# Forgetting attention: values stationary in two parts, turned weights streamed, and the steps of a map regrouped

## Chip, cores and metric

One NeuronCore of a Trainium2 chip runs the whole program in one launch. The metric is device time in microseconds (us). TensorE is the matrix engine (PE in the profile; PEld its weight loads), VectorE is DVE, ScalarE ACT, GpSimd POOL, SyncE SP.

## What is computed

Two transformer blocks over 512 tokens of width 1024 in float32. The change touches one of their mixers, `odd_mixer` of the first block, with 16 heads of 64:

```python
def forgetting_attention(q, k, v, log_f):
    cum = jnp.transpose(jnp.cumsum(log_f, axis=1), (0, 2, 1))
    ...
        s = jnp.einsum('bqhd,bshd->bhqs', qb, k, preferred_element_type=jnp.float32) * scale
        s = s + (cq[..., :, None] - cum[..., None, :])
        p = masked_softmax(s, kpos[None, :] <= tpos[:, None])
        return jnp.einsum('bhqs,bshd->bqhd', p.astype(v.dtype), v)

def odd_mixer(h, w_in, b_f, w_out):
    q, k, v, f = split_cols(h @ w_in, ODD_SPLITS)
    log_f = jax.nn.log_sigmoid((f + b_f).astype(jnp.float32))
    o = forgetting_attention(...)
    return o.reshape(bsz, seq, FOX_W) @ w_out
```

Each query takes a softmax over the keys up to itself, with a bias from the summed log forget gates, and a weighted sum of the values.

## The kernel before

Activations lie transposed: the model's width on 128 partitions in 8 chunks, the 512 tokens along the free axis. Weights stream from memory in panels of 128 x 1024 through a ring. For most of them ScalarE makes a rounded high part (float32r, L567) and VectorE the low part, the rest (L571); a linear layer is then three matmuls of 512 columns for each of 8 chunks (`pe_linear_steps`, L499): high x high, high x low, low x high. `keep_up` (L550) makes the parts two panels ahead.

The stage of the forgetting attention (L1863 to L1971) works so:

- `project` (L934) makes the forget gate and, for each of 8 chunks of two heads, the projections q1, k1 and v1. VectorE drains each bank with the norm's factor (L1007). q1 and k1 are split into high and low parts that are stacked over the partitions (`act_stack_hi` L579, `dve_stack_lo` L585). v1 is turned back to tokens on partitions by four transposes (`pe_turn`, L536) and copied into `v1` by VectorE (L1037).
- The forget gate goes through three activations on ScalarE (`act_f`, L1875) and a scan and six small operations on VectorE (`dve_cum`, L1894) into `parts3`, three bfloat16 parts, whose last mark is called "lo".
- `softmax_maps` (L749) handles 64 maps (16 heads, 4 query tiles of 128). The map of query tile t has (t + 1) x 128 key columns. In step i of its programs TensorE does the scores of map i (two matmuls with stacked parts, then two bfloat16 mask matmuls), the transposes of map i - 2 (one 128 x 128 each key tile), and the value matmuls of map i - 3: turned weights are stationary (128 x 128), values of 64 columns stream, in float32. ScalarE does the turned copy (L812, every other map; VectorE L844 the others) and the exponential with its row sum (L820; the sum is read by an ACTIVATION_READ_ACCUMULATOR). VectorE does the row maximum (L832), the reciprocal of the sum (L837), and scales the output by it (L858). `pe_part` starts after `ready`, the mark "lo".
- Scores and transposes take PSUM banks 3, 4, 5 in turn (`POOLS[1]`), outputs banks 6 and 7 (`POOLS[2]`), projections 0, 1, 2. A bank is taken again once the engine that drained it is done.

`alternate` (L259) weaves the two programs on every engine by one list, `order` (L1969): the first three steps of the projections, then 6 or 9 projection steps to each 8 map steps (a projection has 3 steps, of 9, 9 and 6 matmuls), then what is left of the maps. Each engine works its list strictly in order; nothing but semaphores ties them. The projections run one pair of heads ahead of the maps and so end two heads before them. Afterwards `turned_parts` (L905) turns the output `onat1` by 32 transposes and splits it into `oT1`, and the output projection "mix1" begins (L1973).

## Time and profile before

| | |
|---|---|
| median of 3 runs | 2446.52 us (2444.91 to 2448.24) |
| profiled execution, its own time | 2448.79 us |
| its span in the trace | 2447.0 us |
| PE busy | 2374.6 us, 97% |
| PE weight loads | 1923.7 us, 79% |
| DVE busy | 1424.7 us, 58% |
| ACT busy | 1019.2 us, 42% |
| POOL busy | 273.9 us, 11% |
| mean granted clock of TensorE | 0.991 of full |

The profile is of one execution. Busy time is the union of an engine's instructions; matmuls overlap in the records, so the time that one costs in a stream is the distance from its start to the next one's start, not its recorded duration. In the rows of the trace in order of time, the bracket at the end tells how long the engine sat idle before the row and on whose account. Lines are those of the kernel before.

### The profile page before, as it was taken

To read this page: it belongs to the slowest core of one execution; us is meant where nothing else is said; L and a number is where in the kernel's file an instruction comes from. 1 tells how busy PE (TensorE), PEld (TensorE's weight loads), DVE (VectorE), ACT (ScalarE), POOL (GpSimd) and SP (SyncE) were. 2 spreads that over 40 slices of the span, in tenths; PEclk is the share of its full clock that TensorE was granted. 3 is DMA by queue.
4 is the path that set the end of the run, shared out by engine and by line. 5 is a ranking of instruction groups with operands and counts; after the bars stand their busy time and mean duration, and the time that the engine had idled before them with its cause. 6 is when DMAs were issued, how large, how long until landed. Compare 5 with 4: busy or idle time off the path is not lost.

```text
span 2447.0 us, 32007 instructions
## 1 busy us (share of the span) xinstructions
PE 2374.6 (97%) x12074; PEld 1923.7 (79%) x12086; DVE 1424.7 (58%) x2366; ACT 1019.2 (42%) x1732; POOL 273.9 (11%) x260
## 2 busy tenths in 40 slices
PE   8999899999999999999999999989999998999998
PEld 7877788888887888788888866767888776678887
DVE  3545665655655666566556469947533578666333
ACT  3666664322334444443233344444422354444323
POOL 0000111000001000100000236302100233111001
PEclk8999999999999999999999999999999999999999
DMA  4311002333432111133433312111222221102321
GB/s 180 111 54 44 1 19 104 143 133 129 143 133 87 63 59 61 53 121 129 151 125 136 117 66 70 61 35 36 95 96 97 83 70 61 44 27 75 107 95 52
DMA packets 58039, 211.77 MB, mean 87 GB/s; under 512 B 6432, under 2 KB 6560, under 8 KB 57888
## 3 DMA queue, kind: packets, MB, share of 16 engines
q1 hardware_dynamic: 57456, 208.86, 24.9%
q8 instruction: 99, 1.62, 0.3%
q10 hardware_dynamic: 432, 0.85, 0.1%
q14 instruction: 52, 0.43, 0.1%
HBM read 207.60 MB, written 2.10 MB: 86 GB/s over the span
## 4 chain that ended last, share of the span: by engine, by line
PE 83%; DVE 7%; issue 4%; ACT 4%; POOL 1%; DMA 0%; SPq 0%; ACTq 0%; DVEq 0%; POOLq 0%
PE bank L459 76%; PE last_bank L459 4%; PE bank L469 3%; DVE arena L1146 1%; DVE arena L2233 1%; DVE arena L2235 1%; DVE small L832 1%; ACT wparts L567 1%; ACT arena L820 1%; POOL rstd L626 0%; DMA cb_sb<-cb_dram 0%; DVE arena L2568 0%; DVE wparts L571 0%; ACT arena L2141 0%; DVE arena_r L585 0%
## 5 line engine op out<-in xcount | busy, mean ns | idle before, releaser
L459 PE MATMUL bank<-hT,wparts 128*128 128x512 f32 x5520 | 1334.3, 398 | 6.0 <-DMA cb_sb<-cb_dram 3.5
L459 PEld LDWEIGHTS bank<-hT,wparts 128*128 128x128 f32 x5520 | 1033.6, 190 | 237.4 <-issue 23.2
L571 DVE TENSOR_TENSOR wparts<-ring,wparts 128x1024 fp32r<-128x1024 f32 x290 | 367.3, 1267 | 422.1 <-ACT wparts L567 421.7
L459 PE MATMUL bank<-arena_r,wparts 128*128 128x512 f32 x2400 | 550.5, 390 | 0.0
L459 PEld LDWEIGHTS bank<-arena_r,wparts 128*128 128x128 f32 x2400 | 449.4, 188 | 93.8 <-DVE arena_r L601 0.8
L567 ACT ACTIVATE wparts<-ring 128x1024 fp32r<-128x1024 f32 x332 | 348.2, 1049 | 157.6 <-PE bank L459 124.1
L820 ACT ACTIVATE arena<-bank,small 128x128 f32<-128x128 f32 (+3 forms) x192 | 100.9, 526 | 143.6 <-DVE small L832 142.4
L469 PE MATMUL bank<-cf_sb,arena 128*128 128x128 f32 (+1 forms) x816 | 130.3, 276 | 15.3 <-DMA cf_sb<-cf_dram 5.4
L459 PE MATMUL last_bank<-arena 128*128 128x64 f32 x972 | 131.4, 271 | 9.6 <-DVE arena L855 4.3
L459 PEld LDWEIGHTS last_bank<-arena 128*128 128x128 f32 x972 | 122.4, 192 | 18.8 <-issue 12.6
L832 DVE TENSOR_REDUCE small<-bank 128x1 f32<-128x128 f32 (+3 forms) x192 | 93.4, 487 | 56.7 <-PE bank L459 45.1
L571 POOL TENSOR_TENSOR wparts<-ring,wparts 128x1024 fp32r<-128x1024 f32 x42 | 101.1, 2409 | 213.5 <-ACT wparts L567 213.4
L469 PEld LDWEIGHTS bank<-cf_sb,arena 128*128 128x128 f32 (+1 forms) x816 | 94.5, 145 | 30.9 <-DMA cf_sb<-cf_dram 5.4
L597 ACT ACTIVATE arena_r<-arena 128x512 fp32r<-128x512 f32 x68 | 42.9, 631 | 177.6 <-POOL arena L2792 91.4
L626 POOL TENSOR_TENSOR rstd<-hv 128x512 f32<-128x512 f32 x6 | 7.7, 1291 | 933.8 <-ACT hv L616 933.8
L459 PE MATMUL bank<-arena 128*64 128x128 f32 (+6 forms) x708 | 91.8, 330 | 14.3 <-ACT arena L820 13.9
L812 ACT ACTIVATE arena<-bank 128x384 f32<-128x384 f32 (+3 forms) x136 | 58.0, 426 | 110.3 <-PE bank L469 109.6
L1137 ACT ACTIVATE arena<-arena,vecs 128x512 f32<-128x512 f32 x44 | 35.9, 816 | 147.2 <-DVE arena L1822 147.2
L459 PEld LDWEIGHTS bank<-arena 128*128 128x128 f32 (+2 forms) x708 | 63.6, 170 | 29.9 <-ACT arena L820 16.9
L1146 DVE SCALAR_TENSOR_TENSOR arena<-arena,vecs 128x511 f32<-128x511 f32 x88 | 66.1, 751 | 16.5 <-ACT arena L1137 15.0
L459 PE MATMUL bank<-cb_sb 128*128 128x128 bf16 (+2 forms) x372 | 73.0, 251 | 0.2
L1822 DVE TENSOR_TENSOR arena<-bank,rstd 128x512 f32<-128x512 f32 x44 | 30.4, 691 | 66.4 <-PE bank L459 62.1
(277 smaller groups left out, 2123.3 us busy)
## 6 DMA issues: line engine op xcount, KB each, us to landing
ring<-weights_dram SPq DMA_DIRECT2D x388, 512.0 KB, 3.4
arena<-x_dram SPq DMA_DIRECT2D x4, 512.0 KB, 6.3
out_dram<-arena SPq DMA_DIRECT2D x4, 512.0 KB, 4.0
rot<-rot_dram SPq DMA_DIRECT2D x1, 512.0 KB, 10.9
rot<-rot_dram ACTq DMA_DIRECT2D x1, 512.0 KB, 3.2
cf_sb<-cf_dram SPq DMA_DIRECT2D x1, 416.0 KB, 9.3
cb_sb<-cb_dram SPq DMA_DIRECT2D x1, 264.0 KB, 10.1
vecs<-vec_dram ACTq DMA_DIRECT2D x1, 258.5 KB, 6.3
```

Source lines behind the costliest of these rows:

```text
L459: i = pe.matmul(*args, **kw)
L469: i = pe.transpose(*args)
L567: eng.activation(wparts[:, slot, 0, :, :], ring[:, p % RAW, :, :], ACT.Copy)\
L571: eng.tensor_tensor(wparts[:, slot, 1, :, :], ring[:, p % RAW, :, :], wparts[:, slot, 0, :, :].bitcast(F32), ALU.subtract)\
L597: act.activation(dst, src, ACT.Copy).then_inc(*act_made.mark((key, "hi")))
L812: act.activation(PT[:, j % 3, 0:W], banks[key, "t", j][:, 0:W], ACT.Copy)\
L820: act.activation(Pb[:, i % 3, 0:W], banks[key, "s", i][:, 0:W], ACT.Exp, bias=mx(i), accum_out=sm(i)).then_inc(*act_made.mark((key, "p", i)))
L832: dve.tensor_reduce(mx(i), banks[key, "s", i][:, 0:W], AX.X, ALU.max, negate=True)\
L1137: act.activation(cv, src, ACT.Identity, bias=b, scale=w).then_inc(*act_made.mark((key, "tap", n)))
L1146: dve.scalar_tensor_tensor(out=cv[:, s:SEQ], in0=src[:, 0:SEQ - s], scalar=w, in1=cv[:, s:SEQ], op0=ALU.mult, op1=ALU.add)\
L1822: dve.tensor_tensor(an[:, n % 3, :], banks[(key, "a"), n][:, :], scale, ALU.mult)\
L2233: dve.max(tops[:, r, :], sc).then_inc(*dve_made.mark((K + "top", qt, r)))
```

## The change

Values are now stationary and split. The transposed v1 is copied twice: ScalarE makes its high part (L991 of the new file), VectorE the low part; they lie beside each other (high, low for one head; low, high for the other, `v1[..., 2 * side:2 * side + 2, :]`), in a ring of three chunks. The exponentials are scaled by the reciprocal on GpSimd before they are transposed (`pool_fox`). The turned weights of a head's four maps are split into a high part (ScalarE) and a low part (VectorE) and kept for the whole head. For each head there are then eight matmuls in one bank, two for each key tile kt, with the 128 columns of split values stationary and 512 - 128 kt query columns streamed. The two halves of the bank's partitions hold the parts of the output; ScalarE moves one half across (`swap1`), VectorE adds the other and writes the transposed output `o1`. The turning of the output at the end goes; `oT1` is split from `o1`. Step i is now: transposes of map i - 3, values of a head (where i mod 4 is 3), masks, scores of map i; the other engines treat what TensorE made one step earlier. The exponentials lie in `hv`, the gate's parts in `rstd`.

```diff
@@ project: the values' turning, ScalarE and VectorE @@
+                elif it["kind"] == "turn" and "low" in it:
+                    act.wait_ge(*filled[it["key"], "nat", it["n"]])
+                    if it["free"] is not None:
+                        act.wait_ge(*it["free"])
+                    act.activation(it["dst"], by_head(it["key"], it["n"]), ACT.Copy)\
+                       .then_inc(*act_made.mark((it["key"], "turned hi", it["n"])))
...
+                elif it["kind"] == "turn" and "low" in it:
+                    dve.wait_ge(*act_made[key, "turned hi", n])
+                    dve.tensor_tensor(it["low"], by_head(key, n), it["dst"].bitcast(F32), ALU.subtract)\
+                       .then_inc(*dve_made.mark((key, "turned", n)))
+                    banks.drain((key, "nat", n), "dve_made")
...
-        fox = softmax_maps("fox", maps, Pb1, PT1, lambda i: small_cols(32, i), lambda i: small_cols(36, i, 6),
-                           [dve_made["lo"]], *POOLS[1:])
-        order = [0, 0, 0] + spread(6, 8) + spread(9, 8) * (KD - 2) + [0] + [1] * (len(maps) + 3)
-        then(turned_parts("ot1", onat1, oT1, [dve_made["fox", "out", 63]]))
...
+        def pe_fox(pe):
+            pe.wait_ge(*dve_made["lo"])
+            for i in range(M1 + 5):
+                if 3 <= i < M1 + 3:
+                    j = i - 3
+                    n = j % NT + 1
+                    pe.wait_ge(*pool_made["fox", "scaled", j])
+                    bank = banks.take(pe, ("fox", "t", j), S1)
+                    for t in range(n):
+                        tp(pe, bank[:, t * P:(t + 1) * P], Pb1[:, j % 3, t * P:(t + 1) * P], ident,
+                           done=("fox", "t", j) if t == n - 1 else None)
+                if i >= 7 and i % NT == 3:
+                    h = (i - 7) // NT
+                    c, side = divmod(h, 2)
+                    pe.wait_ge(*dve_made["fox", "lo", NT * h + NT - 1])
+                    pe.wait_ge(*dve_made["v1", "turned", c])
+                    bank = banks.take(pe, ("fox", "o", h), O1)
+                    for kt in range(NT):
+                        values = v1[:, c % VRING, kt, 2 * side:2 * side + 2, :].rearrange("p b d -> p (b d)")
+                        for part in range(2):
+                            last = (kt, part) == (NT - 1, 1)
+                            mm(pe, bank[:, kt * P:SEQ], lhsT=values, rhs=fox_moving(h, part, kt), start=(kt, part) == (0, 0),
+                               stop=last, done=("fox", "o", h) if last else None)
+                if i < M1:
...
+        def act_fox(act):
+            for i in range(M1 + 5):
+                if 3 <= i < M1 + 3:
+                    j = i - 3
...
+                    act.activation(fox_turned(j, 0), turned_map(j), ACT.Copy).then_inc(*act_made.mark(("fox", "hi", j)))
+                if 1 <= i < M1 + 1:
+                    j = i - 1
...
+                    act.activation(Pb1[:, j % 3, 0:W], banks["fox", "s", j][:, 0:W], ACT.Exp, bias=mx1(j),
+                                   accum_out=sm1(j)).then_inc(*act_made.mark(("fox", "p", j)))
+                    banks.drain(("fox", "s", j), "act_made")
+                if i >= 8 and i % NT == 0:
...
+                    act.activation(swap1[HALF[side], :], banks["fox", "o", h][HALF[1 - side], :], ACT.Copy)\
+                       .then_inc(*act_made.mark(("fox", "swap", h)))
+                yield
...
+        def pool_fox(pool):
+            for i in range(M1 + 5):
+                if 2 <= i < M1 + 2:
+                    j = i - 2
+                    p = Pb1[:, j % 3, 0:maps[j]["width"]]
+                    pool.wait_ge(*dve_made["fox", "inv", j])
+                    pool.tensor_scalar(p, p, sm1(j), None, ALU.mult).then_inc(*pool_made.mark(("fox", "scaled", j)))
+                yield
```

`dve_fox` does in step i the maximum of map i - 1, the reciprocal of map i - 2, the low part of the turned map i - 3, and, every fourth step, the sum of a head's halves.

TensorE, in the third pair of heads while projections run; `bank<-arena_r` of 128 to 512 columns are scores, `arena 128x64` values, `L469` transposes, `hT,wparts` projections. Before, two steps:

```order
L459 MATMUL bank<-arena_r 128x384 x2
L459 MATMUL bank<-arena,cb_sb 128x384
L459 MATMUL bank<-cb_sb 128x128
L469 MATMUL bank<-cf_sb,arena 128x128
L459 MATMUL last_bank<-arena 128x64 x4
L459 MATMUL bank<-hT,wparts 128x512 x9
L459 MATMUL bank<-arena_r 128x512 x2
L459 MATMUL bank<-arena,cb_sb 128x512
L459 MATMUL bank<-cb_sb 128x128
L469 MATMUL bank<-cf_sb,arena 128x128 x2
L459 MATMUL bank<-arena 128x64
L459 MATMUL bank<-hT,wparts 128x512 x9
```

Now one step with a head's values between transposes and scores:

```order
L472 MATMUL bank<-cf_sb,hv 128x128
L462 MATMUL last_bank<-arena_r 128x512 x2
L462 MATMUL last_bank<-arena_r 128x384 x2
L462 MATMUL last_bank<-arena_r 128x256 x2
L462 MATMUL last_bank<-arena_r 128x128 x2
L462 MATMUL bank<-rstd,cb_sb 128x512
L462 MATMUL bank<-cb_sb 128x128
L462 MATMUL bank<-arena_r 128x512 x2
L462 MATMUL bank<-hT,wparts 128x512 x9
```

The 64-column matmuls of every step have become one burst in every fourth, ahead of that step's scores.

ScalarE at the start of the stage, before (L579 the stacks of k1, L1877 to L1881 the forget gate):

```order
L579 ACTIVATE arena_r<-arena 64x512 [waits dve_made]
L579 ACTIVATE arena_r<-arena 64x512 x3
L1877 ACTIVATE arena<-arena 16x512 [waits dve_made]
L1879 ACT_TABLE_LOAD
L1879 ACTIVATE arena<-arena 16x512 [waits act_made]
```

and now:

```order
L585 ACTIVATE arena_r<-arena 64x512 [waits dve_made]
L585 ACTIVATE arena_r<-arena 64x512 x3
L991 ACTIVATE arena_r<-bank 128x4x2x64 [waits bank_filled]
L1913 ACTIVATE arena<-arena 16x512 [waits dve_made]
L1915 ACT_TABLE_LOAD
L1915 ACTIVATE arena<-arena 16x512 [waits act_made]
```

The values' high part, which waits for TensorE's transposes, has come ahead of the gate's activations.

VectorE in the same third pair, now (L2086 maximum, L2091 reciprocal, L2095 low part of a turned map, L2102 sum of the halves, L1049 low part of the values):

```order
L2086 TENSOR_REDUCE small<-bank 128x1 [waits act_made,bank_filled]
L2091 RECIPROCAL small<-small 128x1 [waits act_made]
L2095 TENSOR_TENSOR arena_r<-bank,arena_r 128x2x128 [waits act_made]
L2102 TENSOR_TENSOR arena<-bank,hv 64x512 [waits act_made]
L1049 TENSOR_TENSOR arena_r<-bank,arena_r 128x4x128 [waits act_made]
L2086 TENSOR_REDUCE small<-bank 128x1 [waits act_made,bank_filled]
L2091 RECIPROCAL small<-small 128x1 [waits act_made]
```

Between one map's maximum and its reciprocal now lie the low part of an earlier map, the head's sum and the next map's maximum.

## Rows read from the trace of the kernel before

**Rows 1.** The page, busy time, share of the span and instructions of each engine.
```profile
PE 2374.6 (97%) x12074; PEld 1923.7 (79%) x12086; DVE 1424.7 (58%) x2366; ACT 1019.2 (42%) x1732; POOL 273.9 (11%) x260
```

**Rows 2.** Busy time by window: stretch, length, engines, clock, DMA share, GB/s.
```profile
850.00:900.00 50.00, 50.00 (x300) 41.76 (x298) 33.86 (x74) 24.14 (x53) 0.00 (x0) 1.00 0.16 54
```

**Rows 3.** TensorE in order of time, middle: start, length, line, operation, tiles, count.
```profile
851.15 1.00 PE L459 MATMUL last_bank<-arena 128*128 128x64 f32 x8
851.96 2.33 PE L459 MATMUL bank<-hT,wparts 128*128 128x512 f32 x9
854.13 0.62 PE L459 MATMUL bank<-arena_r 128*128 128x512 f32 x2
854.59 0.39 PE L459 MATMUL bank<-arena,cb_sb 96*128 96x512 bf16 x1
```

**Rows 4.** TensorE in order of time, the stage's end.
```profile
982.30 0.65 PE L469 MATMUL bank<-cf_sb,arena 128*128 128x128 f32 x4 [1.12 <-DVE arena L1007]
...
987.83 0.39 PE L459 MATMUL bank<-arena,cb_sb 96*128 96x512 bf16 x1
...
994.71 0.39 PE L459 MATMUL bank<-arena,cb_sb 96*128 96x512 bf16 x1
...
999.74 3.71 PE L469 MATMUL bank<-cf_sb,arena 128*128 128x128 f32 x32 [0.38 <-DVE arena L858]
...
1003.21 12.97 PE L459 MATMUL bank<-arena_r,wparts 128*128 128x512 f32 x56
```

**Rows 5.** VectorE's groups by form, 820 to 980: busy us, mean ns, idle before.
```profile
L585 DVE TENSOR_TENSOR arena_r<-arena,arena_r 64x512 fp32r<-64x512 f32 x36 | 24.7, 686 | 9.3 <-ACT arena_r L579 8.6
L571 DVE TENSOR_TENSOR wparts<-ring,wparts 128x1024 fp32r<-128x1024 f32 x17 | 20.8, 1225 | 12.9 <-ACT wparts L567 12.9
...
L832 DVE TENSOR_REDUCE small<-bank 128x1 f32<-128x512 f32 x11 | 7.6, 692 | 2.3 <-PE bank L459 2.1
L837 DVE RECIPROCAL small<-small 128x1 f32<-128x1 f32 x46 | 7.2, 156 | 0.3
...
L858 DVE TENSOR_SCALAR arena<-bank,small 128x64 f32<-128x64 f32 x23 | 6.4, 277 | 0.0
```

**Rows 6.** ScalarE's groups by form, 820 to 980.
```profile
L579 ACT ACTIVATE arena_r<-arena 64x512 fp32r<-64x512 f32 x36 | 22.5, 626 | 0.6
L567 ACT ACTIVATE wparts<-ring 128x1024 fp32r<-128x1024 f32 x17 | 17.8, 1049 | 0.0
L820 ACT ACTIVATION_READ_ACCUMULATOR arena<-bank,small 128x1 f32 x46 | 8.9, 194 | 0.0
L820 ACT ACTIVATE arena<-bank,small 128x512 f32<-128x512 f32 x11 | 7.6, 689 | 22.3 <-DVE small L832 22.3
...
L812 ACT ACTIVATE arena<-bank 128x384 f32<-128x384 f32 x11 | 5.4, 491 | 11.2 <-PE bank L469 11.2
```

**Rows 7.** Instructions of line 2017: ns min/median/max, first and last start us.
```profile
L2017 POOL TENSOR_SCALAR xT<-xT,vecs x8: 1564/1748/1886, 1458.3 to 1488.6; 128x512 f32<-128x512 f32 x8
```

**Rows 8.** All engines in order of time, the stage's start.
```profile
783.29 0.63 ACT L1877 ACTIVATE arena<-arena 16x512 f32<-16x512 f32 x1
...
785.86 0.66 PE L469 MATMUL bank<-cf_sb,arena 128*128 128x128 f32 x4 [0.79 <-DVE arena L1007]
...
787.18 0.63 ACT L1881 ACTIVATE arena<-arena 16x512 f32<-16x512 f32 x1
...
787.84 0.68 DVE L1896 SCALAR_TENSOR_TENSOR arena<-arena 16x512 f32<-16x512 f32 x1 [0.60 <-ACT arena L1881]
...
792.92 0.44 PE L459 MATMUL bank<-arena_r 128*128 128x128 f32 x2 [0.92 <-DVE arena L1913]
```

**Rows 9.** TensorE in order of time, a wait in the second block.
```profile
1529.38 0.40 PE L459 MATMUL bank<-rstd,cf_sb 16*128 16x64 f32 x2 [3.19 <-DVE arena L1146]
```

**Rows 10.** Busy time by window, the stretch behind that wait.
```profile
1529.40:1533.00 3.60, 3.60 (x12) 2.90 (x13) 3.46 (x14) 2.47 (x7) 2.05 (x1) 0.59 0.00 0
```

**Rows 11.** VectorE in order of time, beside GpSimd's work in the second block.
```profile
1464.56 1.41 DVE L1167 TENSOR_TENSOR arena<-arena,rot 128x512 f32<-128x512 f32 x1
```

More of the change, by code:

```diff
@@ L41 @@
 DSA_EVERY = 4
+VRING = 3
+FOX_STEP = SEQ - P
+FOX_PART = FOX_STEP * (NT - 1) + SEQ
 ALL_BANKS = tuple(range(NBANK))
@@ L1959, in build @@
                     qk=[(qs1[:, at, qt * P:W], kh1[:, at, 0:W]), (qs1[:, at, qt * P:W], kl1[:, at, 0:W])], width=W,
[L1960 to L1963 removed]
+                    masks=[(cstb("selneg")[0:96, h:h + 1].to_broadcast([96, P]), parts3[0:96, 0:W], 0),
+                           (identb, cstb("causal"), qt * P)],
@@ L1971, in build, with mx1, sm1, turned_map @@
-        then(turned_parts("ot1", onat1, oT1, [dve_made["fox", "out", 63]]))
+                            act_made["k1", c, side, "hi", 1 - side])))
+        M1 = len(maps)
+        S1, O1 = POOLS[1:]
+        def mx1(i):
+            return small_cols(32, i)
+        def sm1(i):
+            return small_cols(36, i, 6)
+        def turned_map(i):
+            W = maps[i]["width"]
+            return banks["fox", "t", i][:, 0:W].rearrange("p (t w) -> p t w", w=P)
+        def pe_fox(pe):
[22 more added lines that the diff above has]
+                if i < M1:
+                    m = maps[i]
+                    for w in m["before"]:
+                        pe.wait_ge(*w)
+                    bank = banks.take(pe, ("fox", "s", i), S1)
+                    for n, (a, b, c) in enumerate(m["masks"]):
+                        mm(pe, bank[:, c:c + b.shape[-1]], lhsT=a, rhs=b, start=n == 0, stop=False)
+                    for n, (q, k) in enumerate(m["qk"]):
+                        mm(pe, bank[:, 0:m["width"]], lhsT=q, rhs=k, start=False, stop=n == 1,
+                           done=("fox", "s", i) if n else None)
+                yield
@@ L1972, in build, with act_o1, dve_o1 @@
+        def act_o1(act):
+            act.wait_ge(*filled["fox", "s", M1 - 1])
+            for k in range(KD):
+                act.wait_ge(*dve_made["fox", "out", 2 * k + 1])
+                act_hi(act, oT1[:, 0, k, :], o1[:, k, :], ("ot1", k))
+        def dve_o1(dve):
+            for k in range(KD):
+                dve_lo(dve, oT1[:, 0, k, :], oT1[:, 1, k, :], o1[:, k, :], ("ot1", k))
+        then(act=act_o1, dve=dve_o1)
         f1 = Norm("f1", 1, ("ffn_norm", 1), filled["v1", KD - 1])
```

81 lines of the change are left out of this document (68 added, 13 removed).

## The prediction

> **What bounds the kernel now.** I read the page first: TensorE is busy 97% of the span [rows 1]. Then the stages in the table of windows: in the forgetting-attention stage, while projections run between the heads, it is busy 50.00 of 50.00 us, VectorE 33.86 and ScalarE 24.14, at full clock [rows 2]. So there the sum of TensorE's work sets the time. Then TensorE in order of time through the stage's end: the last block of projection work ends at 982.30, the last two heads follow alone, and the output projection starts at 1003.21 [rows 4]. In that stretch 20.9 us pass and TensorE waits in places: no other work covers the softmax's chain. Last, the stage's beginning: TensorE waits 0.92 us for the forget-gate sums [rows 8]. What the change is worth thus hangs on three places: start, interleaved middle, uncovered end.
>
> **Values: fewer, longer matmuls.** Before, each head has 10 pairs of tiles (query tile by key tile), every one recorded as 2 instructions of 64 columns, 20 in all. Eight of them take from 851.15 to 851.96, 0.10 us each [rows 3]; a head 1.9 to 2.0 us. Now a head has 8 matmuls, two each of 512, 384, 256 and 128 columns, in the same rounded format as the scores. The score pair of 512 takes 0.46 us (854.13 to 854.59) [rows 3]; by columns the four pairs make 0.46 x 1280/512 = 1.15, with a little for the small ones 1.2. Saved: 0.7 us a head, 11 us for 16 heads, all on the engine that bounds the middle. Gone too are the 32 transposes of the output, 3.5 us from 999.74 to 1003.21 [rows 4], but they stand in the uncovered end, where the chain decides. Moving the masks ahead of the scores costs nothing: same matmuls, same bank.
>
> **Other engines.** For each pair of heads VectorE loses a value copy, four turned copies and eight 0.28 us output scalings; it gets the low part of the values, eight low parts of the weights and two sums. Copies, low parts and sums are priced by the nearest row, a 512-wide operation from PSUM at 0.69 [rows 5], about 0.55, 0.4 and 0.28 when narrower. That is 0.69 + 2 x (0.4 + 0.69) + 8 x 0.28 = 5.1 us gone, 0.69 + 2 x 1.92 + 2 x 0.69 = 5.9 added in a period of two heads, 27 us (seven of them from 792.92 to 982.30 [rows 4, 8]): VectorE goes from 68% to some 73%. ScalarE gets four more copies, the values' high part and two moves of 0.63 [rows 6], 3.5 us. GpSimd, idle here, gets eight scalings. Its one row of that form has 1.56 us at least, 1.75 median and 1.89 at most for 512 columns [rows 7]; I take 1.57, and for the narrower maps, between that and a share by columns, 1.2, 0.85, 0.5. None is full. By throughput alone the change gains 11 us.
>
> **The chain is longer.** Before, a map's transposes wait for maximum and exponential only. Now they wait for maximum, exponential, reciprocal and GpSimd's scaling, and each engine's program is in order. In the widest map of a head (512) the path from its scores to its transposes is: 0.2 (TensorE's matmuls are recorded to end 0.16 after the next can start, 0.62 against 0.46 [rows 3]), maximum 0.69 [rows 5], exponential 0.69 + 0.19 [rows 6], then on ScalarE the move of the previous head's half output 0.63, on VectorE the sum that waits for it 0.69, only then the next map's maximum 0.28 and this map's reciprocal 0.16, GpSimd 1.57: 5.1 us, 5.3 with hand-overs of 0.04 (787.18 + 0.63 to 787.84 [rows 8]). The sum stands ahead of the reciprocal in VectorE's program; that is the costly place.
>
> **Middle.** Between those scores and those transposes TensorE has three blocks of projection (two of 9 and one of 6 matmuls: 851.96 to 854.13 is 2.17 for nine [rows 3], so 5.8) and 1.3 of small maps: 7.1 us of cover. But VectorE and ScalarE do the projection's own work in the same queues: the high and low parts of a weight panel (1.05 and 1.23), a drained bank 0.69, and for a key projection four splits of 0.69 [rows 5, 6]. 5.3 + 1.05 + 1.23 + 0.69 = 8.3 against 7.1: a wait of 1.2, more beside the key splits, none where no panel falls between. Laying the steps of one period of two heads out by these durations I get waits of 2 to 3 us in all, most before the transposes of the widest maps, against 1.4 saved. Over seven periods: from -10 (all covered) to +10 (2.9 us of wait each). Where consecutive VectorE instructions overlap a little the waits shrink; I take +0.6 a period, **+4**.
>
> **Start.** The values' high part is now ScalarE's, and its program has it ahead of the three activations of the forget gate. Before, these began at 783.29 and ended at 787.81; the transposes that the high part waits for start at 785.86, so it can begin at 786.5 and end at 787.15, and only then comes the gate's chain. It moves by 3.9 us, and with it VectorE's sums and the first map, for which TensorE waited already [rows 8]: **+3.9**, a wait of 4.8 us. None of it is hidden. After a wait of 3.19 us elsewhere [rows 9] the granted clock of the stretch behind is 0.59 of full over 3.6 us, near the lower level of 1.2 GHz [rows 10]: half speed for about 3.4 us costs 1.7. **+1.7**; ends 0 and 2.
>
> **End.** A cycle of one head without cover, before: 987.83 to 994.71, 6.88 us [rows 4]. After: 5.3 to the end of the scaling, transposes 0.44, +0.2, high part of the turned weights 0.6 (the 384 copy is 0.49 [rows 6]), then ScalarE's next exponential, some 0.47 + 0.19 for 256 columns, which frees the bank for the next transposes, 0.15, the head's value matmuls 1.2, scores of the next widest map 0.75 (0.46 and masks of 512 and 128 columns, a matmul each, 0.29): 9.3 us. Two cycles: +4.8. Drain: before, from the last scores at 995.0 to the output projection 8.2 us; after, 5 to the scaling's end, 0.44, high 0.6, low 0.69, values 1.2, move 0.63, sum 0.69, low part of the first chunk 0.6, hand-overs 0.6: 10.4, so +2.2, although the turning is gone. Entry: TensorE leaves its last projection with the chain about 3 us behind. Together **+10**; ends +6 (scaling at 60% of my price, no swap in the way) and +13 (the clock falls here too).
>
> **Sum:** +4 + 3.9 + 1.7 + 10 = +19.6. The profiled execution took 2448.79 us outside a span of 2447.0; the median shown is 2446.52, 2.3 less. From the median 2466. A measurement can tell 0.2%, about 5 us.
>
> **Rivals.**
> 1. *The middle is covered.* VectorE's 73% leaves room, and a late reciprocal is caught up under three projection blocks. Then -10 + 5.6 + 10 = +6: 2452. It speaks for it that TensorE had no waits in the middle before; against it, that ScalarE and VectorE wait for each other twice per head now.
> 2. *Faster: TensorE binds everywhere.* If the in-order chain keeps pace (it decides at about 4.5 us from scores to transposes, against my 5.3), a head in the end costs TensorE's own 1.2 + 1.1 + 2.2 = 4.5 (values, ten transposes of 0.11, scores with masks) instead of 6.9, -5, and the middle -10, with the start at +3.9: -11, 2436. Against it: GpSimd's row, which no wait shortens.
> 3. *The engines' memory port.* A VectorE instruction with two SBUF inputs of 512 columns took 1.41 us while GpSimd worked [rows 11], and 0.69 in this stage with GpSimd idle [rows 5]. The panel and key splits are of that form and now run beside GpSimd's scalings. Two meetings a period at half a microsecond each add up to 7: 2473. The Trainium skill (SBUF — State Buffer, on the shared port pair) calls it an exclusive lock, held for a whole instruction, against a GpSimd instruction that reads SBUF; by that rule the trace agrees, and it speaks against this change.
> 4. *The change doesn't do what it says:* the values' matmuls cost no less, since each needs its weights loaded anew for a 128 part; 0.7 x 14 more in the middle at worst: 2476.
>
> **Chances.** Forecast 0.49, rival 1 0.17, rival 2 0.14, rival 3 0.13, rival 4 0.07. Faster by over 0.2%: rival 2, 0.14. Within 0.2%: the lower half of rival 1 and a little of rival 2's border, 0.11. Slower 0.75. The forecast's own range is 2458 to 2474; to leave out no more than 2 in 10 it must reach below rival 1, to 2446, and to 2477 above.
>
> **What would show it.** The first map's scores about 4 us later, with TensorE waiting on VectorE for some 4.8 us; behind it a low granted clock. Value matmuls near 1.2 us a head, in one burst. In the middle, waits of TensorE's transposes on GpSimd. At the end about 31 us from the last value transposes to the output projection instead of 20.9, cycles of about 9 us, ScalarE's move and VectorE's sum between the maximum and the reciprocal. The prediction is wrong if the middle shows TensorE without waits and a period near 26, or an end near 21.

## The result, and the profile after

The changed kernel takes **2466.73 us** (median of 4 runs, 2465.69 to 2467.43), the kernel before 2447.38 on the same chip (4 runs, 2444.91 to 2449.39): a ratio of 1.0079, 95% interval 1.0062 to 1.0097, 19.35 us slower. The profiled executions have spans of 2464.5 and 2447.0 us and mean clocks of 0.985 and 0.991. The page of the changed kernel, against [rows 1]:

```profile
PE 2373.0 (96%) x11862; PEld 1915.7 (78%) x11862; DVE 1430.6 (58%) x2350; ACT 1048.0 (43%) x1788; POOL 343.0 (14%) x324
```

The page alone explains nothing: TensorE has 212 instructions fewer and is busy 1.6 us less, although part of its work now runs at the lower clock. So I cut the stage at four places that both traces have: the first value transposes of the stage, the first map's first matmul, the last value transposes, and the first matmul of the output projection.

| stretch | before | after | difference | predicted |
|---|---|---|---|---|
| start: first value transposes to first map | 7.06 (785.86 to 792.92) | 10.94 (783.21 to 794.15) | +3.9 | +3.9 |
| middle: to the last value transposes | 189.38 (to 982.30) | 190.01 (to 984.16) | +0.6, of it 1.5 to 1.7 the low clock | +4, and 1.7 for the clock |
| end: to the output projection | 20.91 (to 1003.21) | 34.62 (to 1018.78) | +13.7 | +10 |
| behind: first stretch of the output projection | 5.76 | 7.67 | +1.9 | 0 |

The low clock's share of the middle is 1.7 by the window below (0.42 of its 4.00 us) and 1.5 by the run e1. The row behind runs from the output projection's first matmul to its first drained bank. The four sum to 20.1. That is more than the 17.5 between the spans because the stage begins 2.65 us earlier in this execution. The program ahead of it is the same; what differs there is the granted clock of the first 100 us, 0.91 before and 0.97 now (in the run e10 it was 0.91 too, and the stage began at 785.25).

**Start.** All engines in order of time; columns: start, length, engine, line, operation, tiles, count, in brackets idle time before and what ended it. Against [rows 8]:

```profile
783.21 0.66 PE L472 MATMUL bank<-cf_sb,arena 128*128 128x128 f32 x4 [0.78 <-DVE arena L1019]
...
783.91 0.60 ACT L991 ACTIVATE arena_r<-bank 128x512 fp32r<-128x512 f32 x1 [3.27 <-PE bank L472]
784.53 0.63 ACT L1913 ACTIVATE arena<-arena 16x512 f32<-16x512 f32 x1
...
788.42 0.63 ACT L1917 ACTIVATE arena<-arena 16x512 f32<-16x512 f32 x1
...
794.15 0.29 PE L462 MATMUL bank<-rstd,cb_sb 96*128 96x128 bf16 x1 [4.82 <-DVE rstd L1949]
...
794.77 3.56 PE L462 MATMUL bank<-hT,wparts 128*128 128x512 f32 x9
```

ScalarE idles 3.27 us for the transposes, then makes the values' high part, then begins the gate at 784.53. TensorE's wait is 4.82 us instead of 0.92. Behind it nine projection matmuls take 3.56 us, where nine took 2.33 [rows 3], and the window says why:

```profile
794.20:798.20 4.00, 4.00 (x14) 3.11 (x15) 3.09 (x4) 0.88 (x3) 0.00 (x0) 0.58 0.39 131
```

(length, busy time of PE, PEld, DVE, ACT, POOL with counts, granted clock, DMA share, GB/s.) The clock is 0.58 of full in this window, where it was 1.00 in the same window before: mostly the lower level, 1.2 GHz.

**Middle.** TensorE in order of time, the end of a head's values, its next widest scores, and the transposes of that map; this answers to [rows 3]:

```profile
966.63 1.47 PE L462 MATMUL last_bank<-arena_r 128*128 128x512 f32 x8
967.94 0.39 PE L462 MATMUL bank<-rstd,cb_sb 96*128 96x512 bf16 x1
...
968.74 2.25 PE L462 MATMUL bank<-hT,wparts 128*128 128x512 f32 x9
...
971.39 1.61 PE L462 MATMUL bank<-hT,wparts 128*128 128x512 f32 x6
...
973.63 2.21 PE L462 MATMUL bank<-hT,wparts 128*128 128x512 f32 x9
976.48 0.66 PE L472 MATMUL bank<-cf_sb,hv 128*128 128x128 f32 x4 [0.64 <-POOL hv L2113]
```

The eight value matmuls hold TensorE for 1.31 us (966.63 to 967.94) instead of 1.9. The transposes of the widest map wait 0.64. TensorE's waits from 796 to 984 (us, times, longest); before, there were two waits of 1.4 us together, both in the first heads (801.82 and 803.31), and none from there to 982:

```profile
PE bank L472 <- POOL hv L2113: 8.7, 14, 1.4
```

A period of two heads is 27.83 before and 27.76 now. In a steady period TensorE idles twice, 0.45 and 0.64 us. The run e3 below, without any of these waits, has a period of 26.26: TensorE's own work fell by 1.57 us a period, and the waits put 1.50 back, 0.4 more than the records show as idle time. Of the work saved, the bursts are 0.6 us a head. The rest is about what the projections gain: nine of their matmuls hold TensorE for 2.09 us behind scores (968.74 to 970.83), where behind 64-column matmuls it was 2.17 [rows 3], six times a period.

**End.** TensorE from the last value transposes on, against [rows 4]:

```profile
984.16 0.66 PE L472 MATMUL bank<-cf_sb,arena 128*128 128x128 f32 x4 [0.79 <-DVE arena L1019]
...
995.68 0.39 PE L462 MATMUL bank<-rstd,cb_sb 96*128 96x512 bf16 x1
...
998.83 0.88 PE L472 MATMUL bank<-cf_sb,hv 128*128 128x128 f32 x3 [1.63 <-ACT hv L2074]
...
1001.75 1.12 PE L472 MATMUL bank<-cf_sb,hv 128*128 128x128 f32 x4 [1.19 <-POOL hv L2113]
...
1004.28 2.14 PE L462 MATMUL bank<-arena_r 128*128 128x512 f32 x8
1006.26 0.39 PE L462 MATMUL bank<-rstd,cb_sb 96*128 96x512 bf16 x1
...
1013.95 2.61 PE L462 MATMUL last_bank<-arena_r 128*128 128x512 f32 x8 [1.41 <-DVE arena_r L2095]
1018.78 1.62 PE L462 MATMUL bank<-arena_r,wparts 128*128 128x512 f32 x3 [2.22 <-DVE arena_r L607]
```

A head's cycle without cover is 10.58 us (995.68 to 1006.26) instead of 6.88. Inside it, VectorE, ScalarE and GpSimd on the widest map and the head's sum:

```profile
996.68 0.69 DVE L2086 TENSOR_REDUCE small<-bank 128x1 f32<-128x512 f32 x1 [2.36 <-PE bank L462]
...
997.41 0.69 ACT L2065 ACTIVATE hv<-bank,small 128x512 f32<-128x512 f32 x1
...
998.21 0.59 ACT L2074 ACTIVATE hv<-last_bank 64x512 f32<-64x512 f32 x1
...
998.83 0.69 DVE L2102 TENSOR_TENSOR arena<-last_bank,hv 64x512 f32<-64x512 f32 x1 [1.06 <-ACT hv L2074]
...
999.56 0.29 DVE L2086 TENSOR_REDUCE small<-bank 128x1 f32<-128x128 f32 x1
...
999.88 0.16 DVE L2091 RECIPROCAL small<-small 128x1 f32<-128x1 f32 x1
...
1000.14 2.14 POOL L2113 TENSOR_SCALAR hv<-hv,small 128x512 f32<-128x512 f32 x2 [1.36 <-DVE small L2091]
```

The order is as predicted: maximum, exponential, ScalarE's move, VectorE's sum, the next map's maximum, and only then the reciprocal that GpSimd waits for. From the widest maximum's start to the transposes 5.07 us pass (996.68 to 1001.75), and from the end of its scores (996.48) 5.27, against 5.3 in the prediction. The last row joins two scalings, 512 columns and the 128 of the next map. And the clock, in the end and behind it:

```profile
984.16:1018.78 34.62, 20.04 (x89) 15.54 (x90) 14.43 (x37) 14.45 (x37) 11.42 (x10) 0.71 0.00 0
1018.78:1061.00 42.22, 42.22 (x178) 34.76 (x179) 22.62 (x27) 18.02 (x28) 6.50 (x5) 0.95 0.27 88
```

Before, both clocks were 1.00. In shorter windows the clock falls behind the wait of 2.86 us before 988.23 (0.54 from 988.23 to 995.68), is back at 1.00 from 995.68, falls again behind the wait of 1.63 (0.51 from 998.83 to 1001.75), is back at 1.00 from 1006.26, and is 0.50 from 1013.95 to 1022.50, behind waits of 1.97, 1.92 and 1.41. Before the change, waits of up to 1.12 us stood in this stretch. Now 89 matmuls take 20.04 us of the end; four transposes 1.12 us instead of 0.66, eight value matmuls 2.14 instead of 1.47.

### The profile page after: what moved, and what is told of

Its sections match the earlier page's. It is cut to its first block, busy times and chain, and to the rows that moved or that the text cites. A ratio compares the mean times of both kernels' runs of the same rounds, so it can differ in the third digit from the quotient of the medians.

```text
span 2464.5 us, 31535 instructions
## 1 busy us (share of the span) xinstructions
PE 2373.0 (96%) x11862; PEld 1915.7 (78%) x11862; DVE 1430.6 (58%) x2350; ACT 1048.0 (43%) x1788; POOL 343.0 (14%) x324
## 4 chain that ended last, share of the span: by engine, by line
PE 82%; DVE 7%; issue 5%; ACT 4%; POOL 2%; DMA 0%; SPq 0%; ACTq 0%; DVEq 0%; POOLq 0%
PE bank L462 75%; PE last_bank L462 4%; PE bank L472 3%; DVE arena L1163 1%; POOL hv L2113 1%; DVE arena L2392 1%; DVE arena L2394 1%; ACT wparts L573 1%; POOL rstd L632 0%; ACT arena L826 0%; DVE small L838 0%; DVE arena L1019 0%; DMA ring<-weights_dram 0%; DVE small L2086 0%; DVE arena L2727 0%
## 5 line engine op out<-in xcount | busy, mean ns | idle before, releaser
L462 PE MATMUL last_bank<-arena 128*128 128x64 f32 x780 | 107.0, 273 | 8.0 <-DVE arena L861 4.4
L462 PEld LDWEIGHTS last_bank<-arena 128*128 128x128 f32 x780 | 99.3, 194 | 16.7 <-issue 11.5
L472 PE MATMUL bank<-cf_sb,arena 128*128 128x128 f32 (+4 forms) x624 | 99.7, 280 | 11.6 <-DMA cf_sb<-cf_dram 5.0
L826 ACT ACTIVATE arena<-bank,small 128x256 f32<-128x256 f32 (+3 forms) x128 | 67.2, 525 | 73.4 <-DVE small L838 72.8
L2113 POOL TENSOR_SCALAR hv<-hv,small 128x128 f32<-128x128 f32 (+1 forms) x64 | 69.3, 1083 | 180.0 <-DVE small L2091 180.0
L472 PEld LDWEIGHTS bank<-cf_sb,arena 128*128 128x128 f32 (+4 forms) x624 | 74.9, 148 | 23.0 <-DMA cf_sb<-cf_dram 5.0
L462 PE MATMUL bank<-arena 128*64 128x128 f32 (+6 forms) x580 | 74.0, 346 | 14.3 <-ACT arena L826 13.6
L838 DVE TENSOR_REDUCE small<-bank 128x1 f32<-128x256 f32 (+3 forms) x128 | 62.3, 487 | 40.3 <-PE bank L462 39.3
L818 ACT ACTIVATE arena<-bank 128x256 f32<-128x256 f32 (+3 forms) x104 | 45.7, 439 | 70.1 <-PE bank L472 69.4
L607 DVE TENSOR_TENSOR arena_r<-arena,arena_r 128x512 fp32r<-128x512 f32 x76 | 53.1, 707 | 35.6 <-ACT arena_r L603 35.4
```

Of the source, the lines that this page charges most:

```text
L462: i = pe.matmul(*args, **kw)
L472: i = pe.transpose(*args)
L607: dve.tensor_tensor(lo, src, hi.bitcast(F32), ALU.subtract).then_inc(*dve_made.mark((key, "lo")))
L818: act.activation(PT[:, j % 3, 0:W], banks[key, "t", j][:, 0:W], ACT.Copy)\
L826: act.activation(Pb[:, i % 3, 0:W], banks[key, "s", i][:, 0:W], ACT.Exp, bias=mx(i), accum_out=sm(i)).then_inc(*act_made.mark((key, "p", i)))
L838: dve.tensor_reduce(mx(i), banks[key, "s", i][:, 0:W], AX.X, ALU.max, negate=True)\
```

## The experiments

Each is an edit of the changed kernel. "Ratio" is to the kernel before on the same chip, with its 95% interval; the changed kernel's own is 1.0079. The runs e1 to e4 stood beside a kernel before of 2445.59 us, e5 to e8 of 2449.60, e9 and e10 of 2449.24, so of two medians the ratios tell more than the difference. The intervals of e1, e2, e4, e5 and e7 overlap that of the changed kernel: what such an edit gives back is read from the stretches of its trace, one execution each, and the medians only agree with it. The last columns are read from each run's trace as in the table above: the first to the last value transposes (start and middle together), a period of two heads, and the end.

| run | median us | ratio | start and middle | period | end |
|---|---|---|---|---|---|
| kernel before | 2447.38 | 1 | 196.44 | 27.83 | 20.91 |
| changed kernel | 2466.73 | 1.0079 | 200.95 | 27.76 | 34.62 |
| e1 gate first | 2461.35 | 1.0059 (1.0040 to 1.0079) | 195.53 | 27.75 | 35.81 |
| e2 sum late | 2460.41 | 1.0061 (1.0040 to 1.0082) | 196.35 | 26.98 | 30.77 |
| e3 no scaling | 2453.64 | 1.0032 (1.0022 to 1.0041) | 191.54 | 26.26 | 30.26 |
| e4 warm end | 2460.45 | 1.0059 (1.0039 to 1.0080) | 200.97 | 27.74 | 31.05 |
| e5 VectorE scales in the end | 2463.29 | 1.0073 (1.0048 to 1.0098) | 202.05 | 27.75 | 30.12 |
| e6 VectorE scales | 2458.14 | 1.0045 (1.0029 to 1.0062) | 193.31 | 26.26 | 32.54 |
| e7 scores first | 2467.01 | 1.0083 (1.0067 to 1.0098) | 202.57 | 27.83 | 35.80 |
| e8 together | 2446.80 | 0.9994 (0.9984 to 1.0003) | 186.79 | 26.30 | 27.49 |
| e9 together, warm end | 2442.36 | 0.9969 (0.9956 to 0.9982) | 186.76 | 26.30 | 25.20 |
| e10 distances of before | 2454.98 | 1.0026 (1.0016 to 1.0035) | 197.57 | 27.85 | 24.63 |

### e1: the gate ahead of the values' high part

The gate's activations and sums are run before the first value item's copies instead of after them.

```diff
                            free=filled["fox", "o", 2 * (c - VRING) + 1] if c >= VRING else None,
+                           **(dict(act2=act_f, dve2=dve_cum) if c == 0 else {}))]
...
-        then(act=act_f, dve=dve_cum)
```

> Only the start changes: ScalarE does the forget gate's activations, and VectorE its sums, before the two parts of the first turned values. Theory (the start's order costs 3.9 us of wait and 1.7 us of low clock): the wait before the first map's masks falls from 4.82 us to about 1, the granted clock stays full behind it, and the whole runs 5 to 6 us faster than the changed kernel, some 2461. Rival (the wait is taken back later, because the middle is bound by the other engines' chain and TensorE would wait there anyway): the start gets 4 us shorter and the middle 4 us longer, 2466.

```profile
783.41 0.63 ACT L1917 ACTIVATE arena<-arena 16x512 f32<-16x512 f32 x1
783.94 0.57 ACT L991 ACTIVATE arena_r<-bank 128x512 fp32r<-128x512 f32 x1
...
789.14 0.23 PE L462 MATMUL bank<-rstd,cb_sb 96*128 96x128 bf16 x1 [0.94 <-DVE rstd L1949]
```

The wait before the first map is back at 0.94 and start and middle together are 5.4 us shorter: 3.9 of chain and 1.5 of clock, 5.6 predicted. The period doesn't move. In this execution the end is 1.2 longer, at a clock of 0.62; the median is 5.4 lower (4.9 by the ratios) all the same. The start's term stands, in the traces.

### e2: the sum of the halves one map later

```diff
-            for i in range(M1 + 5):
+            for i in range(M1 + 6):
...
-                if i >= 8 and i % NT == 0:
-                    h = (i - 8) // NT
+                if i >= 9 and i % NT == 1:
+                    h = (i - 9) // NT
```

(In VectorE's program alone; ScalarE's move stays.)

> VectorE's sum of a head's two halves moves one step later, behind the next reciprocal. Theory (the sum, waiting for ScalarE's move, holds up the reciprocal and with it GpSimd's scaling of the widest map): that map's scaling starts about 1.3 us earlier, the waits of TensorE on GpSimd in the middle (8.7 us, 14 times) nearly go, the end gets 2 to 3 us shorter; together 8 to 11 us, some 2457. Rival (GpSimd's own 1.56 us and the longer path as such are what costs; the queue order only shifts the wait): less than 2 us.

No work is taken away, only its place in one queue: 4.6 us less in the middle (the waits on GpSimd go from 8.7 to 4.9), 3.9 less in the end, the median 6.3 lower (4.4 by the ratios; the profiled execution was the fastest of the five). The forecast of 8 to 11 us was too high: about half of the waits went. Part of the end's 3.9 is the clock, 0.77 in it against 0.71. But the place that I had called costly is costly: the sum, itself waiting for ScalarE's move, stood ahead of the reciprocal.

### e3: no scaling

```diff
-                    pe.wait_ge(*pool_made["fox", "scaled", j])
+                    pe.wait_ge(*act_made["fox", "p", j])
...
-                if 2 <= i < M1 + 2:
+                if False:
```

> GpSimd's scaling of the exponentials is left out (the attention output is not divided by its row sums) and the transposes wait for the exponential alone. Theory (the chain with GpSimd in it takes back what the values save): the waits on GpSimd in the middle go, so the period of two heads falls from 27.76 to about 26.5, 8.7 us in all; in the end each of the two cycles loses at least the 1.56 us and part of the wait for the reciprocal, 5 us or more; 2450 or below. Rival (the values' matmuls don't save what they should, and the middle is bound by TensorE's work): middle as it is, only the end gains, 2461.

This leaves out the division by the row sums. The period falls to 26.26, 1.57 below before. From 820 to 965 us TensorE has no wait in either, so all of it is TensorE's own work: 0.8 a head, against the 0.7 predicted. The end keeps 9.4 of its 13.7, at a low clock again (0.73). So GpSimd's scaling, with the wait for the reciprocal ahead of it, takes back nearly all that the middle gains, and is a third of what the end loses. In the median the run is 13.1 us faster than the changed kernel (11.5 by the ratios; 16 or more expected).

### e4: TensorE kept busy in the end

At eight places of the end, constant matmuls into a bank that nobody reads, 57 in all, ahead of TensorE's waits.

```diff
+WARM = {("t", 54): 10, ("t", 55): 5, ("t", 58): 7, ("t", 59): 5, ("t", 62): 8, ("t", 63): 8, ("o", 15): 6, "end": 8}
...
+                    pe_busy(pe, banks["v1", KD - 1], WARM.get(("t", j), 0))
...
+                    pe_busy(pe, banks["v1", KD - 1], WARM.get(("o", h), 0))
...
+                if i == M1 + 4:
+                    pe_busy(pe, banks["v1", KD - 1], WARM["end"])
```

> While TensorE waits in the stage's end (before eight of its waits) it does 5 to 10 matmuls of constants into a bank that nobody reads, 57 in all; nothing else changes. Theory (the end costs 10 us by its chain, and the rest of the 13.7, and 1.9 behind it, is the low clock, 0.71 in the end and 0.95 behind it): clock 1.00 in both, end about 31 us instead of 34.6, mix1's first stretch 1.9 shorter, 4 to 6 us faster, some 2461. Rival (the end is all chain; the clock falls where TensorE waits anyway): no gain, 2466, or a loss where the extra matmuls outlast a wait.

```profile
984.03:1015.08 31.05, 26.45 (x143) 16.01 (x147) 14.31 (x37) 14.77 (x37) 11.44 (x10) 1.00 0.00 1
1015.08:1056.00 40.92, 40.92 (x181) 33.86 (x181) 22.61 (x27) 18.63 (x28) 6.97 (x6) 1.00 0.27 90
```

With the clock at 1.00 throughout, the end takes 31.05 us, 10.1 more than before, and TensorE still waits on ScalarE and GpSimd in it. That splits the end's +13.7: 10.1 of chain (at most, since the added matmuls can outlast a wait), 3.6 of clock, and 1.9 of clock behind. A head's cycle is 9.49 us here (994.18 to 1003.67), and from the last scores (1004.48) to the output projection 10.60. The median is 6.3 lower (4.9 by the ratios). Work added at no use to the result makes the kernel faster.

### e5 and e6: VectorE scales instead of GpSimd

From map 53 on (e5), or for all maps (e6).

```diff
+DVE_SCALES = 53
...
+                    if j >= DVE_SCALES:
+                        p = Pb1[:, j % 3, 0:maps[j]["width"]]
+                        dve.wait_ge(*dve_made["fox", "inv", j])
+                        dve.tensor_scalar(p, p, sm1(j), None, ALU.mult).then_inc(*dve_made.mark(("fox", "scaled", j)))
...
-                if 2 <= i < M1 + 2:
+                if 2 <= i < M1 + 2 and i - 2 < DVE_SCALES:
```

(e6 has 0 in the first line; TensorE waits for the engine that scaled.)

> From map 53 on, that is in the uncovered end alone, VectorE scales the exponentials instead of GpSimd; the middle is the changed kernel's. Theory (in the end GpSimd's 1.56 us is on the path of every widest map, two cycles and the drain, and behind a narrower scaling in its queue): the end gets 3 to 5 us shorter, near that of the run without any scaling (30.3 us), some 2462. Rival (what the run without scaling gained in the end came from the reciprocal's wait, not from GpSimd's duration; VectorE's own queue takes as long): 1 us or less.

> VectorE scales the exponentials everywhere, GpSimd has nothing to do in the stage. Theory (TensorE waits for the time from scores to transposes, not for an engine that is full): although VectorE gets eight more operations a period, about 3 us, on top of some 19 of 27, the waits before the transposes shrink and a period falls from 27.76 to 26.5 or 27; with the end as in the run that changes only the end, 8 to 12 us faster, 2456. Rival (VectorE is near its limit and its order binds): the period stays or grows, 2462 or more.

The same scaling on both engines, groups by form (busy us, mean ns of one, idle before); GpSimd in the changed kernel from 820 to 980, then VectorE in e6 from 820 to 960:

```profile
L2113 POOL TENSOR_SCALAR hv<-hv,small 128x512 f32<-128x512 f32 x12 | 18.8, 1563 | 24.5 <-DVE small L2091 24.5
...
L2113 POOL TENSOR_SCALAR hv<-hv,small 128x128 f32<-128x128 f32 x12 | 7.2, 603 | 13.8 <-DVE small L2091 13.8
```

```profile
L2096 DVE TENSOR_SCALAR hv<-hv,small 128x512 f32<-128x512 f32 x11 | 5.4, 487 | 0.4
...
L2096 DVE TENSOR_SCALAR hv<-hv,small 128x128 f32<-128x128 f32 x11 | 3.2, 288 | 0.4
```

e6 has the same period as e3, which doesn't scale at all: on VectorE the scaling is free in the middle, though it is the busier engine. Start and middle are 7.6 us shorter, the end 2.1, and the median is 8.6 lower (8.3 by the ratios), as far as forecast. In e5 the end is 4.5 shorter, part of it clock (0.77 against 0.71), but in its profiled execution the low clock behind the start lasted longer (start and middle are 1.1 longer), and its interval takes in both no gain and all that was hoped for: inconclusive by the median.

### e7: masks and scores ahead of a head's values

TensorE issues a map's masks and scores before the previous head's value matmuls, so that the value burst leaves the cycle of the chain. The diff moves the ten lines from `if i < M1:` on; nothing else changes.

> In the steps that have a head's value matmuls, TensorE does the masks and scores of the next head's widest map before them, not behind them. Theory (in the end the value matmuls, with their wait for the last low part, stand in the cycle between one widest map's transposes and the next one's scores): each of the two cycles gets 2 to 2.6 us shorter, the end falls from 34.6 to 30 or 31, the middle gains 1 or 2 us since the widest map has 1.3 us more cover; some 2460. Rival (the values come later by as much, and ScalarE's move and VectorE's sum behind them hold the next reciprocal longer): nothing, or slower.

It gains nothing (27.83 a period, an end of 35.80, median +0.3). The end's clock was 0.67 against 0.71, but TensorE's busy time in it the same (20.08 and 20.04), so no gain hides there, and the middle at full clock moved by nothing either. The trace shows where the gain went:

```profile
995.41 0.69 DVE L2086 TENSOR_REDUCE small<-bank 128x1 f32<-128x512 f32 x1 [0.89 <-PE bank L462]
...
996.99 0.41 PE L472 MATMUL bank<-cf_sb,hv 128*128 128x128 f32 x2
...
997.44 0.38 ACT L2058 ACTIVATE arena_r<-bank 128x256 fp32r<-128x256 f32 x1 [2.69 <-PE bank L472]
...
997.72 0.68 ACT L2065 ACTIVATE hv<-bank,small 128x512 f32<-128x512 f32 x1
```

The widest maximum now runs beside the value burst, but its exponential starts 2.31 us behind it (995.41 to 997.72), where in the changed kernel it was 0.73 (996.68 to 997.41). ScalarE's program has the high part of an earlier map (L2058) ahead of that exponential, and the transposes for it come behind the burst. So the edit did not take the burst out of the cycle, it only moved the place where the chain meets it, and my theory is neither borne out nor tested by it.

### e8 and e9: the edits together

e8 is e1, e2, e6 and e7 in one; e9 adds 44 constant matmuls in the end's waits, as e4 does.

> The gate first, the sum one step later, the scores before the values, and the scaling on VectorE, all four. Theory (the losses are waits that these take away one by one, and the values' saving of about 0.6 us a head then shows): start 5.5 us, middle 9 us or a little more, end down to 24 or 25 us with the clock near full: 2440 to 2446, level with the kernel before or below it. Rival (they take away the same waits twice, and VectorE becomes the bound): 2450.

> The run with all four edits, plus matmuls of constants in TensorE's waits of the end (44 in all, sized by that run's waits). Theory (the low clock costs its own share in the end and behind it): no low clock from 960 to 1060, end 27.5 us down to 24 or 25, 2 us less behind it, 4 to 5 us faster than the four edits alone, 2441 to 2443, and that would be below the kernel before. Rival (the end is bound by the chain between the other engines, TensorE's speed does not count): 2446 as without.

e8 stands level with the kernel before; its end of 27.49 missed the 24 or 25 expected, at a clock of 0.79. e9 is **faster than both**, than the kernel before by 0.3%: 0.9969 (0.9956 to 0.9982). Its windows, a middle one and the end:

```profile
850.00:900.00 50.00, 50.00 (x276) 41.74 (x275) 42.22 (x90) 31.49 (x69) 0.00 (x0) 1.00 0.17 58
969.02:994.22 25.20, 23.25 (x133) 14.70 (x134) 18.18 (x47) 14.59 (x37) 0.00 (x0) 1.00 0.01 1
```

TensorE has no gap in that middle window, as before the change [rows 2], with VectorE 8.4 us busier. Start and middle are 9.7 us shorter than before; the end is still 4.3 longer. At full clock the end is 31.05 in e4 and 25.20 in e9: the later sum, VectorE's scaling and the order of e7 are together worth 5.9 us of it. What is left over the kernel before, 4.3, no run takes apart. So the split values pay in the middle once the chain around them is placed; over the whole kernel they come out level (e8), and ahead by 0.3% with the constant matmuls (e9). e9 is 0.25% below e8, by ratios: the warm end again.

### e10: the other engines not one step behind

With e1 and VectorE's scaling, the distances of the kernel before: maxima and exponentials in the map's own step, transposes two steps after the scores, values at `i % NT == 2`, and, as there, the scores ahead of the transposes in TensorE's step. Of the edit:

```diff
-                if 3 <= i < M1 + 3:
-                    j = i - 3
+                if 2 <= i < M1 + 2:
+                    j = i - 2
...
-                if 1 <= i < M1 + 1:
-                    j = i - 1
+                if i < M1:
+                    j = i
```

> The gate first and the scaling on VectorE, but the distances of the kernel before: in step i the scores of map i, the transposes of map i - 2, a head's values where i mod 4 is 2; maximum and exponential in the step of their scores. Theory (the extra step of distance buys nothing, since TensorE's wait is for the path from scores to transposes, and in the uncovered end every step of distance puts more of the other engines' work into their queues ahead of it): middle at 26.3 a period as with the other distance, end shorter than 27.5 us, 24 or less; 2443. Rival (the distance is what lets the middle run without waits, as the change says): the middle shows waits of TensorE again, period 27 or more, 2450.

```profile
PE bank L473 <- DVE arena L1020: 3.1, 5, 0.6
PE bank L473 <- DVE hv L2099: 2.9, 7, 0.4
PE bank L473 <- DVE arena_r L2103: 2.2, 2, 1.3
```

Those are TensorE's waits from 796 to 978, on the drain, the scaling and the low part; the last two lie in the first heads, each of the others comes once a period. The period is 27.85, though scaling by VectorE alone had brought it to 26.26: the extra step of distance is what lets the longer chain hide in the middle, as the rival said, and my 26.3 for it was wrong (2454.98 us instead of 2443). In the end it is the other way: 24.63 us at a clock of 0.85, against 32.54 at 0.72 in e6, and 27.49 at 0.79 even in e8, which has the later sum too. Part of these differences is clock, but e9, at full clock, still takes 25.20. Where nothing covers the chain, a step of distance is a step more to drain. A version with distance in the middle and without it in the end wasn't tried.

## Why the prediction was right, and where two errors met

**Right: the sign, the three places, and what each costs there.** Forecast 2466.0, measured 2466.73.

- **Start.** +3.9 predicted and measured, a wait of 4.82 against "some 4.8". The low clock behind it came, 1.7 predicted; e1 gives back 5.4 for both, 1.5 of it clock. The step "half speed for about 3.4 us" was a little high by its own row: 0.59 of full over 3.6 us [rows 10] loses 0.41 x 3.6 = 1.5. The row of the wait of 3.19 us in another block [rows 9, 10] was a good enough neighbour.
- **Values.** 1.2 us a head predicted, 1.31 measured. Eight matmuls in four widths stay a little above the rate of the 512 pair, which would make 1.15. By e3's period TensorE's work fell by 0.8 a head, where the step "Saved: 0.7 us a head" had 0.7; the burst itself is 0.6 of it, and the shorter blocks of projections, which I had not foreseen, make up about the rest. Rival 4 is out.
- **End, the chain.** +10 predicted, +10.1 measured at full clock (e4), and its parts too: a cycle 9.3 predicted, 9.49 in e4; the drain 10.4 predicted, 10.60. e2 shortened the end by 3.9, e3 and e5 by 4.4 and 4.5. These overlap, because e3 takes the reciprocal's wait away with the scaling, and each has some clock in it. What the later sum, VectorE's scaling and e7's order are worth together at full clock is 5.9 (e4 against e9).
- **VectorE's load.** "From 68% to some 73%" doesn't follow from its own terms: 5.9 - 5.1 = 0.8 us in a period of 27 is 3 points, 71%. It measured 35.09 us of 50, 70% (850 to 900). The period itself was 27.83, not 27: seven of them don't fit from 792.92 to 982.30, where the first heads are shorter. Nothing in the sum hung on either.

**Wrong in size: the middle.** The step "5.3 + 1.05 + 1.23 + 0.69 = 8.3 against 7.1" put every piece of projection work of a period into the path of the widest map, and "waits of 2 to 3 us in all" was its result; measured were 8.7 us in 7 periods, 1.2 a period (1.1 in a steady one). VectorE, ScalarE and GpSimd on the way to the transposes at 976.48:

```profile
969.14 1.40 DVE L591 TENSOR_TENSOR arena_r<-arena,arena_r 64x512 fp32r<-64x512 f32 x2 [1.07 <-ACT arena_r L585]
...
973.09 0.69 DVE L2102 TENSOR_TENSOR arena<-last_bank,hv 64x512 f32<-64x512 f32 x1 [0.99 <-ACT hv L2074]
...
973.81 0.69 DVE L1019 SCALAR_TENSOR_TENSOR arena<-bank,rstd 128x512 f32<-128x512 f32 x1
...
974.87 1.56 POOL L2113 TENSOR_SCALAR hv<-hv,small 128x512 f32<-128x512 f32 x1 [2.18 <-DVE small L2091]
```

The cover is just the 7.1 that I had (968.74 to 975.84, where the wait starts), but the path from there to the transposes is 7.74, not 8.3: two key splits stand in it (1.40 on VectorE) and a drain of 0.69, while the panel's high and low part (975.09 on ScalarE, 976.17 on VectorE) come after the exponential and the reciprocal. The term was +4; without the clock the middle came out at -0.9 to -1.1, so 5 too high, nearly all of it because a steady period changed by -0.07 and not by +0.6. Rival 1, "the middle is covered", is half true: it is not covered, but it is level.

**Wrong in size: the end's clock.** "The clock falls here too" stood only at the range's end of +13. It did fall, and cost 3.6 in the end and 1.9 behind it, 5.5 too low; the end's +13.7 lies even beyond that +13. The one row I had was a wait of 3.19 us; here it fell behind one of 2.86 and, between short pieces of work, behind one of 1.63.

The two errors, +5 and -5.5, cancel. The hit on the number, 0.7 us off, is luck to that extent; either alone would have missed by 5 us, within the range.

**Rival 2** (TensorE binds everywhere) is out: from the widest maximum to the transposes the end takes 5.07 us, also at full clock (e4, 995.19 to 1000.26), above its limit of 4.5.

**Rival 3** (the memory port) is out in this stage, more by absence than by test. It needed two meetings a period between VectorE's splits, which read two operands from SBUF, and GpSimd's scalings. By the trace of all splits from 796 to 984 (42 of the keys, 20 of the panels) they hardly meet: a panel split begins 0.26 us before a scaling ends, once a period, and a single key split lies wholly beside one. VectorE and GpSimd in order of time there:

```profile
809.32 1.56 POOL L2113 TENSOR_SCALAR hv<-hv,small 128x512 f32<-128x512 f32 x1 [2.94 <-DVE small L2091]
...
810.20 2.83 DVE L591 TENSOR_TENSOR arena_r<-arena,arena_r 64x512 fp32r<-64x512 f32 x4 [0.52 <-ACT arena_r L585]
```

The first of these four lies beside the scaling, which ends at 810.88, and neither gets longer: four splits with GpSimd idle take 2.84 (from 951.11), another scaling of 512 columns 1.56. Nor did the groups' means move, 1226 ns for a panel split and 686 for a key split, against 1225 and 686 [rows 5]. The Trainium skill (SBUF — State Buffer, on the shared port pair) has an exclusive lock for such a pair; this one meeting shows neither engine held, and here the measurement decides. It is one meeting, but the kernel before has more, in the stretch of [rows 11]:

```profile
1463.03 2.39 POOL L571 TENSOR_TENSOR wparts<-ring,wparts 128x1024 fp32r<-128x1024 f32 x1
...
1476.31 1.57 POOL L2017 TENSOR_SCALAR xT<-xT,vecs 128x512 f32<-128x512 f32 x1
...
1477.44 0.68 DVE L1167 TENSOR_TENSOR arena<-arena,rot 128x512 f32<-128x512 f32 x1
```

The 1.41 from 1464.56 lay beside GpSimd instructions of two operands (L571 to 1465.42, then L2015). Beside a scaling, the form that this change adds, the same VectorE instruction took 0.68 at 1477.44, its first 0.44 us in the scaling, and 0.88 at 1470.80, wholly beside one. So the row that the rival was priced from had another partner; a scaling cost at most 0.2. What in the partner makes the difference, no run here tests.

## What to carry to other kernels

When a step is added to a chain, write down each engine's queue in program order and look for an instruction that waits for another engine and stands ahead of one that the chain needs: moving such a one by a step adds no work and gave back 4 to 6 us in the medians here (e2, with an interval that still overlaps the changed kernel's). A chain hides behind other work in the middle of a stage and not at its ends, so price the uncovered start and end separately, with the clock in the price; extra distance between steps pays in the first place and costs in the second. And try a cheap elementwise step first on the engine that is faster at it, even if that is the busier one, as long as it has room (VectorE 42.22 of 50 us in e9).

## What the hardware showed that I had not expected

- The granted clock fell in a stretch whose single waits were only 1.2 to 2.9 us, with TensorE busy 20.04 of 34.62 us; it was 0.71 there and 0.95 in the 42 us behind. 57 constant matmuls put it back to 1.00. In the traces that is worth 5.5 us (3.6 and 1.9), in the medians 5 to 6.
- Scaling 512 columns in place by a value per partition takes 1.56 us on GpSimd and 0.49 on VectorE; 128 columns 0.60 and 0.29.
- Nine projection matmuls hold TensorE for 2.17 us behind 64-column float32 matmuls and 2.09 behind scores, both at full clock.
- A wait's named releaser can be the wrong one. TensorE's wait of 2.86 us before 988.23 is put down to ScalarE's move, which its transposes don't need; the move ends at 988.19, GpSimd's scaling of that map, which they do need, at 988.17 (986.93 and 1.24).
